# A depthwise convolution of 31 taps moved from TensorE to GpSimd and VectorE in a two-layer decoder step

## The reference, cut to what matters

```
z = x @ w_in                                   # (L, 2576)
A: y_a = B * conv3(C * h)                      # 256 channels
B: gated linear attention, chunks of tokens     # 4 heads
C: c_full = concat(hist_c, c_a * sigmoid(c_g))  # 256 channels, 30 tokens of history
   y_c = silu(layer_norm(causal_dwconv(c_full, c_conv_w) + c_conv_b, c_ln_g, c_ln_b))
D: gMLP with a 128 x 128 spatial matrix
x = LN(ALPHA * x + concat(y_a, y_b, y_c, y_d) @ w_out)      # LN1
x = LN(ALPHA * x + relu(x @ w_ff1)^2 @ w_ff2)               # LN2, w_ff1 is 1024 x 4096
```

## Time and profile before

| | before |
|---|---|
| median of 3 runs | 1771.22 us (1771.35, 1771.22, 1747.97) |
| the profiled execution's own time | 1745.49 us |
| its span, slowest core (core 0) | 1743.9 us (all cores 1716.3 to 1743.9) |
| mean granted clock of core 0 | 0.960 |
| PE busy | 1563.0 us, 90% |
| DVE busy | 890.5 us, 51% |
| ACT busy | 759.6 us, 44% |
| POOL busy | 163.2 us, 9% |

### The profile page before, as it was taken

One profiled execution on the slowest core, in us unless ns is written; L12 is line 12 of the kernel. 1 busy time (PEld: TensorE's weight loads), 2 busy tenths in 40 slices (PEclk: granted clock), 3 DMA queues, 4 the chain that ended last, 5 costly groups with the idle time before them and its releaser, 6 DMA issues.

```text
span 1743.9 us, 27641 instructions; the slowest of 8 cores (1716.3 to 1743.9 us)
## 1 busy us (share of the span) xinstructions
PE 1563.0 (90%) x9070; PEld 848.6 (49%) x9214; DVE 890.5 (51%) x1984; ACT 759.6 (44%) x1467; POOL 163.2 (9%) x188
## 2 busy tenths in 40 slices
PE   5578998788999989898999989999999999968995
PEld 3344454344444545455565544545454544535562
DVE  4647343376218545685334843476336656484215
ACT  3243343336343433644346442545355524634343
POOL 1001101010001130010100210000001030010001
PEclk9888999898999998999999999999999999988998
DMA  9998999984997598464786778983456354332332
GB/s 173 152 231 199 177 202 224 225 228 142 195 216 250 127 212 171 140 194 103 162 227 180 230 163 196 237 258 111 166 177 197 143 166 143 97 118 97 121 123 83
DMA packets 133931, 303.38 MB, mean 174 GB/s; under 512 B 48144, under 2 KB 98704, under 8 KB 109840
## 3 DMA queue, kind: packets, MB, share of 16 engines
q1 hardware_dynamic: 81248, 244.93, 44.2%
q0 software_dynamic: 52544, 56.69, 24.2%
HBM read 289.37 MB, written 76.48 MB: 210 GB/s over the span
## 4 chain that ended last, share of the span: by engine, by line
PE 75%; DMA 7%; issue 6%; ACT 6%; DVE 4%; POOL 1%; another core or an unknown queue 1%; DVEq 0%; ACTq 0%; POOLq 0%; SPq 0%
PE pst L48 75%; DMA s_xbM<-xb 2%; DVE scr L48 2%; ACT s_ymix L48 1%; DMA scr<-stc 1%; DVE s_acc L48 1%; DMA s_mr<-w_in 1%; DMA s_fr<-w_ff 1%; DMA s_mr<-wc 1%; ACT L48 1%; ACT s_xbF L48 1%; ACT scr L48 1%; ACT s_sring L48 1%; ACT s_junk L48 1%
## 5 line engine op out<-in xcount | busy, mean ns | idle before, releaser
L48 PE MATMUL pst<-s_xbF,s_fr 128*128 128x512 bf16 (+3 forms) x2782 | 501.7, 338 | 22.7 <-ACT s_xbF L48 12.5
L48 PE MATMUL pst<-s_fr,s_hbuf 128*128 128x512 bf16 x2053 | 467.0, 381 | 14.5 <-ACT s_hbuf L48 9.0
L48 DVE SCALAR_TENSOR_TENSOR s_acc<-s_acc,pst 128x512 f32<-128x512 f32 x340 | 232.8, 686 | 345.8 <-PE pst L48 339.0
L48 PEld LDWEIGHTS pst<-s_xbF,s_fr 128*128 128x128 bf16 x2816 | 276.2, 100 | 224.9 <-issue 31.5
L48 PEld LDWEIGHTS pst<-s_fr,s_hbuf 128*128 128x128 bf16 x2112 | 204.3, 98 | 252.1 <-issue 22.5
L48 ACT ACTIVATE s_sring<-pst 128x512 f32<-128x512 f32 (+3 forms) x324 | 162.4, 502 | 304.9 <-PE pst L48 291.1
L48 PE MATMUL pst<-s_xbM,s_mr 128*128 128x512 bf16 (+2 forms) x1252 | 237.9, 350 | 15.8 <-DMA s_xbM<-xb 4.5
L48 ACT ACTIVATE scr<-pst 128x512 f32<-128x512 f32 (+7 forms) x260 | 119.8, 471 | 264.0 <-PE pst L48 223.5
L48 ACT ACTIVATE s_hbuf<-s_sring 128x512 bf16<-128x512 f32 (+3 forms) x311 | 164.9, 530 | 31.8 <-DVE s_sring L48 2.4
L48 DVE SCALAR_TENSOR_TENSOR s_acc<-s_acc,s_fst,s_lng 128x1024 f32<-128x1024 f32 x136 | 173.0, 1281 | 10.8 <-POOL s_fst L48 9.2
L48 PEld LDWEIGHTS pst<-s_xbM,s_mr 128*128 128x128 bf16 (+1 forms) x1280 | 108.3, 98 | 125.8 <-issue 21.6
(11 more groups left out here) (130 smaller groups left out, 1092.4 us busy)
## 6 DMA issues: line engine op xcount, KB each, us to landing
s_fr<-wc SPq DMA_DIRECT2D x118, 1024.0 KB, 6.2
s_mr<-wc SPq DMA_DIRECT2D x27, 1024.0 KB, 8.7
wc<-s_fr SPq DMA_DIRECT2D x26, 1024.0 KB, 10.6
s_fr<-w_ff POOLq DMA_DIRECT2D x22, 1024.0 KB, 17.4
x<-s_acc SPq DMA_DIRECT2D x17, 512.0 KB, 7.3
s_acc<-x SPq DMA_DIRECT2D x17, 512.0 KB, 5.5
s_acc<-xp SPq DMA_DIRECT2D x16, 512.0 KB, 8.1
wc<-w_ff POOLq DMA_DIRECT2D x8, 1024.0 KB, 15.8
```

The lines of the kernel that those rows point to most:

```text
L48: return lambda e: getattr(e, name)(*a, **k)
```

## The change

Passes 0 and 1 of layer 0 (`NPEC = 2`) keep the convolution on PE. In the other six (`tapped`):

- `conv_in` runs first in the mixer: the projections of part C, the gated product `gC` (not folded, 512 tokens in one piece, kept in the memory of `diagC`), and for the prompt tokens the convolution on POOL: for each of 2 channel halves one TENSOR_SCALAR (product plus bias) and 30 times a TENSOR_SCALAR (product, to `ctm`) and a TENSOR_TENSOR (sum, to `cacc`), each of 128x512. That is 62 TENSOR_SCALAR and 60 TENSOR_TENSOR a pass.
- the sample's 128 tokens get their taps on DVE: 2 TENSOR_SCALAR and 60 SCALAR_TENSOR_TENSOR of 128x128, twice in the program.
- `conv_out` runs last, after part D: the layer norm over channels (in pieces of 512 columns, `onesa`) and Silu.
- POOL's convolution operations are marked `back`: the planner takes one only when nothing else is ready on POOL (at costs of 650 and 1050 in its own unit). `MSTART` goes from -0.1 to -0.2.
- `diagC` is no longer built for layer 1; the constants move (`cvp`, `tcv`).

```diff
-MSTART = -0.1
+MSTART = -0.2
+NPEC = 2
@@ schedule
+                    if o.back:
+                        k += 1e6
@@ emit_M
+            tapped = l > 0 or S >= NPEC
+            def conv_in():
...
+                for j in range(2):
+                    P.add("pool", I("tensor_scalar", cacc.c(j * NT, nP), gC.c(j * LD, nP), tcv(j * 31), tcv(62 + j), ALU.mult, ALU.add),
+                          kg(j) + cvec.k(), kc(j), cost=650.0).back = True
+                for k in range(1, 31):
+                    for j in range(2):
+                        P.add("pool", I("tensor_scalar", ctm[j].c(0, nP), gC.c(j * LD + k, nP), tcv(j * 31 + k), None, ALU.mult),
+                              kg(j) + cvec.k(), ctm[j].k(), cost=650.0).back = True
+                    for j in range(2):
+                        P.add("pool", I("tensor_tensor", cacc.c(j * NT, nP), cacc.c(j * NT, nP), ctm[j].c(0, nP), ALU.add),
+                              ctm[j].k() + kc(j), kc(j), cost=1050.0).back = True
+                if has_s:
...
+                    for k in range(1, 31):
+                        for j in range(2):
+                            P.dve(I("scalar_tensor_tensor", av(j), sv(j, k), tcv(j * 31 + k), av(j), ALU.mult, ALU.add),
+                                  kgs(j) + cvec.k() + ks(j), ks(j), 128)
+            if tapped:
+                conv_in()
...
-            for f in ((mixer_d, mixer_c) if S == 0 and l == 0 else (mixer_c, mixer_d)):
-                f()
+            if tapped:
+                mixer_d()
+                conv_out()
+            else:
+                for f in ((mixer_d, mixer_c) if S == 0 and l == 0 else (mixer_c, mixer_d)):
+                    f()
```

More of the change, by code:

```diff
@@ L18 @@
 EPS = 1e-5
-NCV = 149
+NCV = 77
+NCP = 140
+NPEC = 2
 GR = 64
@@ L513, in build_program @@
         onesb = mk("onesb", 128, BF16)
+        onesa = mk("onesa", 128, BF16)
+        stg_p = mk("stg_p", 60, F32)
         trilb = mk("trilb", 128, BF16)
@@ new lines, in conv_out @@
+            def conv_out():
+                ar = Arena(0)
+                cb16 = ar.carve(2 * 512, BF16)
+                csq = ar.carve(2 * 512, BF16)
+                mean = ar.carve(512, F32)
+                msq = ar.carve(512, F32)
+                rstd = ar.carve(512, F32)
+                tmpn = ar.carve(2 * 512, F32)
+                for (t0, n, kind) in TT:
+                    for j in range(2):
+                        v = cacc.c(j * NT + t0, n)
+                        kv = cacc.k(j * NT + t0, j * NT + t0 + n)
+                        P.either(I("activation", csq.c(j * 512, n), v, AF.Square),
+                                 I("tensor_tensor", csq.c(j * 512, n), v, v, ALU.mult), kv, csq.k(j * 512, j * 512 + 512), n)
+                        P.either(I("activation", cb16.c(j * 512, n), v, AF.Copy),
+                                 I("tensor_copy", cb16.c(j * 512, n), v), kv, cb16.k(j * 512, j * 512 + 512), n, 0.52)
+                    inv = 1.0 / 256.0
+                    p1, p2 = mbank(), mbank()
+                    for src, pb in ((cb16, p1), (csq, p2)):
+                        P.pe([mm(pb.c(0, n), onesa.c(0, 128), src.c(j * 512, n), n, j == 0, j == 1) for j in range(2)],
+                             onesa.k() + src.k(), pb.k())
+                    P.either(I("activation", mean.c(0, n), p1.c(0, n), AF.Copy, scale=inv),
+                             I("tensor_scalar", mean.c(0, n), p1.c(0, n), inv, None, ALU.mult), p1.k(), mean.k(), n)
+                    P.act(I("activation", msq.c(0, n), p1.c(0, n), AF.Square, scale=inv), p1.k(), msq.k(), n)
+                    P.dve(I("scalar_tensor_tensor", rstd.c(0, n), p2.c(0, n), inv, msq.c(0, n), ALU.mult, ALU.subtract),
+                          p2.k() + msq.k(), rstd.k(), n)
+                    P.act(I("activation", rstd.c(0, n), rstd.c(0, n), AF.Ln, bias=cEPS.c(0, 1), scale=1.0), rstd.k() + cEPS.k(), rstd.k(), n, AF.Ln)
+                    P.act(I("activation", rstd.c(0, n), rstd.c(0, n), AF.Exp, scale=-0.5), rstd.k(), rstd.k(), n, AF.Exp)
+                    for j in range(2):
+                        kv = cacc.k(j * NT + t0, j * NT + t0 + n)
+                        kt = tmpn.k(j * 512, j * 512 + 512)
+                        t_ = tmpn.c(j * 512, n)
+                        P.dve(I("tensor_tensor", t_, cacc.c(j * NT + t0, n), mean.c(0, n), ALU.subtract), kv + mean.k(), kt, n)
+                        P.dve(I("tensor_tensor", t_, t_, rstd.c(0, n), ALU.mult), kt + rstd.k(), kt, n)
+                        P.act(I("activation", ymix.c((4 + j) * XS + t0, n), t_, AF.Silu, bias=tcv(66 + j), scale=tcv(64 + j)),
+                              kt + cvec.k(), ky(4 + j, t0, n), n, AF.Silu)
@@ L1486, in _cvec @@
     cw = np.asarray(inp["c_conv_w"][l], np.float32)
+    for j in range(2):
+        cols.append(cw[:, j * 128:(j + 1) * 128].T)
+    for name in ("c_conv_b", "c_ln_g", "c_ln_b"):
+        cols.append(fm(inp[name][l], 2))
     for g in range(4):
@@ L1500, in _cvec @@
     out = np.concatenate(cols, axis=1)
-    assert out.shape == (128, NCV), out.shape
+    assert out.shape == (128, NCV + NCP), out.shape
     return out
```

107 lines of the change are left out of this document (97 added, 10 removed).

## The result

| | before | after |
|---|---|---|
| median | 1771.28 us (4 executions) | 2147.39 us (2142.22 to 2237.84) |
| ratio, 95% interval | | 1.219 (1.200 to 1.239) |
| span of the profiled execution, its slowest core | 1743.9 us | 2140.7 us |
| granted clock of that core | 0.960 | 0.872 |

The kernel became 22% slower, 376 us. Slower was forecast, but at 1812 us; the range ended at 1880.

The account below looks back on a forecast made before the run. TensorE was taken to bound the interiors, TensorE and VectorE together the boundaries. Against the profiled 1745.5 us: -50 + 66 + 30 + 8 = +54, 1799.5, plus 13 toward the median: 1812 us, range 1722 to 1880.

Parts of the forecast that it names:

- The price of the product: GpSimd's TENSOR_SCALAR of 128x512: priced at 0.65 us, between a MEMSET's 0.525 and a TENSOR_TENSOR's 1.05 us.
- The rival at 1.05 us: GpSimd's TENSOR_SCALAR costs as much as its sum, 1.05 us: +74 us, 1886 us in all; chance 0.1.
- The sum: GpSimd's TENSOR_TENSOR of the convolution: priced at 1.05 us by the s_tokm row; a skill-based estimate was 1.12 us.
- The total fits, that wait costs nothing: GpSimd's 103 us of convolution fits a pass of about 200 us; conv_out's wait is free if it ends within some 190.
- The four boundaries: LN2-to-LN1 stretches at 740, 957, 1153, 1333 us: convolution ahead of the last pow lengthens them, together +66 us.
- The blocking: Where VectorE and GpSimd both read SBUF, they exclude each other for one instruction's length; 0.28 us overlaps per alternation.
- TensorE's -50 us: Diagonal matmuls of six passes leave interiors where TensorE sets the time: 50 us saved, bounds 40 and 60.
- The sample's taps, +30 us: Twice 60 VectorE operations of 128x128 in interiors, slowed by GpSimd: +15 us each time, bounds 0 and 34 each.
- The clock, +8 us: TensorE's granted clock falls after new waits at the four boundaries: +8 us, bounds 0 and 16.
- Casting loads late, +20 us as a rival: Pass (S 0, l 1): eight weight loads queue behind GpSimd's convolution, +20 us, 1832 us; counted within the main case's range.
- MSTART, counted at nothing: Lower MSTART and conv_in first move mixer work earlier: counted at nothing, perhaps 10 us either way.

Follow-up runs that it names:

- e3: The kernel after, with a second operation (plus constant 0) in GpSimd's 360 products, same order: 1984.7 us, ratio 1.134 to before.
- e6: The kernel after, with two-operation products and the planner told the measured costs of 0.86 and 1.36 us: 1924.7 us, ratio 1.100.
- e7: As e6, but a pass's convolution may not start on GpSimd before the last pow of LN1 of the pass beside it: 2008.0 us, ratio 1.146.
- e2: The kernel after, with the prompt's taps 1 to 30 left out on GpSimd, all else of the change kept: 1730.4 us, ratio 0.987.
- e9: As e6, with GpSimd's products and sums replaced by MEMSETs of 710 and 1380 elements, which read nothing: 1807.3 us, ratio 1.037.
- e4: The kernel after, with GpSimd's products and sums replaced by MEMSETs of 1500 and 1230 elements, which read nothing: 2044.4 us, ratio 1.165.
- e1: The kernel before plus a series of single GpSimd forms after its last store, some beside VectorE sums: one-operation product 1.56 us, two-operation 0.69 or 0.76.
- e8: The kernel after, without the sample's taps 1 to 30 on VectorE in the last passes: 2127.4 us, ratio 1.215.
- e11: As e6, but only the four passes of layer 1 convolve on GpSimd; layer 0 keeps its diagonal matmuls: 1857.5 us, ratio 1.065.
- e13: As e6, with a MEMSET of 8 elements on GpSimd after every tap's two sums: 1883.0 us, ratio 1.077.
- e14: As e6, with a MEMSET of 8 elements on GpSimd after every product and every sum: 1895.6 us, ratio 1.081.

## Why the prediction was wrong, step by step

Lengths of the boundaries from first to last pow, as in the forecast, and the rest of the time up to the last pow, in us, from the traces:

| | 365 | 529 | 744 | 958 | 1153 | 1333 | 1534 | rest |
|---|---|---|---|---|---|---|---|---|
| before | 44 | 39 | 49 | 47 | 40 | 42 | 47 | 1428 |
| after | 45 | 41 | 84 | 80 | 71 | 76 | 46 | 1689 |
| e3 two operations | 44 | 41 | 77 | 70 | 62 | 64 | 48 | 1568 |
| e6 | 50 | 53 | 67 | 62 | 55 | 54 | 46 | 1527 |
| e7 gated | 36 | 41 | 53 | 52 | 36 | 37 | 46 | 1693 |
| e2 no taps | 39 | 40 | 51 | 46 | 41 | 50 | 46 | 1412 |

- **The price of the product: wrong, and the first step that failed.** "One operand and one output is nearer to the first: 0.65 us". The bounds were 0.525 and 1.05; the chip takes 1.56, above both. The interpolation isn't what failed, since the form with two operations takes 0.69: both rows that I had were of other operations, and neither could bound this one. The rival at 1.05 us was in the right direction and too small. With the product at 0.84 us and nothing else changed (e3) the kernel takes 1985 us, so this step is worth 163 us and is not the whole error.
- **The sum: 1.05 us forecast, 1.25 measured.** The Trainium skill (GPSIMD Engine Reference, "Elementwise — side-by-side cycle accounting") led to an estimate of 1.12 us; the measurement lies above that as well.
- **"The total fits, that wait costs nothing": wrong, and the dearer step.** A convolution of 178 us is below the 190 that I had allowed, but GpSimd has some 19 us more to do in a pass ((1220.4 - 1066.3) / 8), and a pass lasted 195 us before: no room was left, and GpSimd is busy 93% of an interior. The table shows where that went: 262 us outside the boundaries, 135 in them. The forecast's own sum with the right durations, about 1910 us, would have been 237 us short. Even where the load fits (e9) the queue costs 77 us. My reading is that the mixer's own pows and products, the next `conv_in` and `conv_out` all wait in a fixed order; in the kernel after VectorE waits 58 us for the mixer's rows on GpSimd and 95 us for `gC`, and which of these waits makes up the 262 us was not told apart. I had priced the operations inside four boundaries only. Ahead of the first boundary 117 stood too, and the first interval grew by 97 us (161 to 462 against 161 to 365), of which 47 are there without the taps as well (161 to 411 in e2).
- **The four boundaries: mechanism right.** Forecast +13, +16, +19, +18. In the kernel after it was 35, 33, 31, 34; the forecast's own sum with 1.56 and 1.25 us gives 40, 40, 43, 43. e3 has the same order: its boundaries grew by 28, 22, 23 and 22, in sum 95, where the forecast's sum with 0.69 and 1.25 us gives 88. e6 grew by 60, but holds 34 to 37 operations a boundary and not 43 to 47, so that it lies near the forecast's 66 is chance. (Two slips in that sum: the first boundary was taken from 740 us, 53 us long, and is 49 from first to last pow; the term at 957 comes to 16.7, not 16.)
- **The blocking: right that it exists, wrong in its length.** Norms of 1.63 us and taps of 0.71 were as named. "For the length of one instruction" is wrong: a norm of 1.28 us lasts up to 5.17 in the kernel after, and with the fast product a VectorE instruction lasts 19.59 us (e6). The Trainium skill (SBUF — State Buffer, "Who interferes with whom") says that whoever issues first has the shared pair for the whole instruction, and that a VectorE instruction with two inputs in SBUF is held up by one of GpSimd only if that one reads SBUF; e4 and e1's MEMSETs agree with the second part, while the first doesn't foresee a waiting instruction that is passed by twenty.
- **TensorE's -50 us: right as busy time, open as time.** Matmuls with diagC are 128, as expected, and busy 16 us where they were 67. e2, with all the rest of the edit, was forecast at 1725 to 1745 and took 1730, but that forecast holds -50 for the matmuls and +30 for the taps, and only their sum was measured: -25 against its own kernel before.
- **The sample's taps, +30 us:** 81 us busy in the kernel after, and 20 us less without them (e8), not clear of the noise. In e2, where GpSimd is idle, they take 0.35 us each; what they cost there was not measured.
- **The clock, +8 us: too small.** TensorE's busy time is 1596 us against 1549 in e2, which has the same matmuls, at a granted clock of 0.872 against 0.942: 47 us. It came with 364 us more of idle TensorE than before; I had priced four short waits.
- **Casting loads late, +20 us as a rival:** TensorE waits 10.2 us for `s_fr<-w_ff` where it waited 3.7; a small term.
- **MSTART, counted at nothing:** 29 us in favour of the change as it stands, at the edge of the noise.

## What to carry to other kernels

Price an operation by its own form: where the trace has none, the rows of other operations are no bounds, and the size of the load decides whether "it fits" is true. An engine at 9% is still in the path if others wait for its small operations, so count what stands ahead of each of them over the whole program, not only at the places that look full. Where VectorE and GpSimd both read SBUF, a stream without gaps on GpSimd can hold VectorE up for many instructions; a short operation that reads nothing, once in five, was cheap here. And when a version is built to leave one thing out, look whether the planner kept the order: e3 can be compared with the kernel after term by term, e4 and e9 can't.

## What the runs showed of the hardware that was not expected

- GpSimd's TENSOR_SCALAR of 128x512 to float32 takes 1.56 us with a product alone and 0.69 us with a second operation that adds 0. The slow form disturbs VectorE less (0.92 us a sum against 1.02 and 0.77 alone). That would fit if part of its length is no reading; no run tests it further.
- A float32 sum on GpSimd beside a float32 sum on VectorE doubles the latter (0.77 to 1.50 us) and slows itself (12.94 / 8 = 1.62 us against 4.07 / 3 = 1.36).
- A VectorE instruction that waits for reads can be passed by GpSimd's many times when these run without a gap; the longest was 19.59 us for 0.69 us of work. All such cases of 17 us and more stand beside products of 0.69 us and their sums (e3, e6, e7, e11); beside products of 1.56 us none lasted over 5.2 us (the slowest core of each run). With an operation between the taps that only writes, the longest was 3.24 us (e13), with one after every operation 4.12 (e14).
